# Two transformer blocks in one kernel: unscaled probabilities in the second attention, a new order in the delta rule, the conv products and the third pair's scores

## The reference

```python
# first block, delta rule, per head and chunk of 64 tokens
lower = bc[..., None] * jnp.einsum('nbhid,nbhjd->nbhij', kc, kc) * dec_strict
sol = lax.linalg.triangular_solve(lower + jnp.eye(C), rhs, left_side=True, lower=True, unit_diagonal=True)
...
o = rmsnorm(o, norm_w) * jax.nn.silu(z.reshape(B, S, H, dv))
# first block, sparse attention (8 heads, window, selected and compressed branches)
o = gates[..., 0:1] * o_cmp + gates[..., 1:2] * o_slc + gates[..., 2:3] * o_win
# second block
p = jax.nn.softmax(logits, axis=-1)              # 8 heads of 64, causal, with a bias by distance
attn_out = p @ v
u = a * jax.nn.sigmoid(g)                        # 512 channels
u = lax.conv_general_dilated(u, w_dw[:, None, :], ..., feature_group_count=C) + b_dw   # 31 taps, causal
mixed = jnp.concatenate([attn_out, layernorm_silu(u)], axis=-1)
h = h + mixed @ w_out[l]
```

## Time and profile before

| | us |
|---|---|
| median of three timed runs | 1605.27 (1605.24 to 1605.73) |
| profiled execution | 1607.56 |
| its span | 1605.8 |
| PE busy in the span | 1529.8 |
| DVE, ACT, POOL busy | 867.0, 641.9, 212.6 |

### The profile page before, as it was taken

The page is one execution under the profiler, slowest core; times in us unless marked ns, Lnnn a source line. Parts: engine busy times, 40 slices in busy tenths (PEclk is TensorE's granted clock), DMA queues, the critical chain, the costliest instruction groups (busy, mean ns, idle before and its releaser), DMA issues. The chain is left out here.

```text
span 1605.8 us, 21770 instructions
## 1 busy us (share of the span) xinstructions
PE 1529.8 (95%) x8438; PEld 1247.9 (78%) x8438; DVE 867.0 (54%) x1300; ACT 641.9 (40%) x936; POOL 212.6 (13%) x191
## 2 busy tenths in 40 slices
PE   6997999999999899999999998989799999999998
PEld 5777978667888777888888876767578888888886
DVE  5755446673444477766732266677626444444222
ACT  5354422463223244443422155454635444443221
POOL 0004000681000000000000001378610000000000
PEclk9999999999999999999999998999979999999999
DMA  5210032001223313233232233122103223222321
GB/s 211 79 53 16 2 142 101 21 1 40 98 93 110 105 53 103 81 104 104 69 115 90 91 123 105 53 79 79 30 24 105 91 92 104 99 83 73 104 94 71
DMA packets 22534, 132.17 MB, mean 82 GB/s; under 512 B 2480, under 2 KB 2864, under 8 KB 12224
## 3 DMA queue, kind: packets, MB, share of 16 engines
q1 hardware_dynamic: 20672, 123.48, 22.8%
q0 software_dynamic: 928, 6.36, 1.0%
q10 hardware_dynamic: 864, 1.36, 0.2%
HBM read 129.09 MB, written 2.10 MB: 82 GB/s over the span
## 5 line engine op out<-in xcount | busy, mean ns | idle before, releaser
L322 PE MATMUL ps<-AH,whi 128*128 128x512 f32 x1280 | 509.6, 398 | 39.1 <-DVE wlo L309 14.6
L323 PE MATMUL ps<-AL,whi 128*128 128x512 f32 x1280 | 504.8, 394 | 0.0
L324 PE MATMUL ps<-AH,wlo 128*128 128x512 f32 x1280 | 504.3, 394 | 0.0
L309 DVE TENSOR_TENSOR wlo<-raw,whi 128x2048 fp32r<-128x2048 f32 (+3 forms) x124 | 251.2, 2026 | 272.0 <-ACT whi L302 271.8
L322 PEld LDWEIGHTS ps<-AH,whi 128*128 128x128 f32 x1280 | 244.7, 191 | 95.9 <-issue 21.9
L324 PEld LDWEIGHTS ps<-AH,wlo 128*128 128x128 f32 x1280 | 244.3, 191 | 52.0
L323 PEld LDWEIGHTS ps<-AL,whi 128*128 128x128 f32 x1280 | 244.5, 191 | 50.4 <-issue 0.2
L302 ACT ACTIVATE whi<-raw 128x2048 fp32r<-128x2048 f32 (+3 forms) x124 | 210.3, 1696 | 169.9 <-PE ps L324 169.9
L322 PE MATMUL ps<-HH,whi 128*128 128x512 f32 x352 | 136.9, 389 | 0.0
L323 PE MATMUL ps<-HL,whi 128*128 128x512 f32 x352 | 136.9, 389 | 0.0
L324 PE MATMUL ps<-HH,wlo 128*128 128x512 f32 x352 | 136.9, 389 | 0.0
(11 more groups left out here) (384 smaller groups left out, 1928.9 us busy)
## 6 DMA issues: line engine op xcount, KB each, us to landing
raw<-wstream SPq DMA_DIRECT2D x78, 1024.0 KB, 4.8
raw<-wstream SPq DMA_DIRECT2D x32, 704.0 KB, 4.1
raw<-wstream SPq DMA_DIRECT2D x16, 768.0 KB, 4.3
hT<-xT SPq DMA_DIRECT2D x4, 512.0 KB, 7.9
raw<-wstream SPq DMA_DIRECT2D x4, 512.0 KB, 3.6
W1k<-w1k_d POOLq DMA_DIRECT2D x1, 2048.0 KB, 10.7
W1v<-w1v_d POOLq DMA_DIRECT2D x1, 2048.0 KB, 15.9
BT<-bias_d POOLq DMA_DIRECT2D x1, 1024.0 KB, 5.6
```

Of the source, the lines that this page charges most:

```text
L309: nc.vector.tensor_tensor(WL[b][:, 0:n], RAW[b][:, 0:n], WH[b][:, 0:n].bitcast(F32), ALU.subtract).then_inc(w_lo_done, 1)
L322: nc.tensor.matmul(out_, WH[b][:, w], xh[:, k, :], start=start and k == 0, stop=False)
L323: nc.tensor.matmul(out_, WH[b][:, w], xl[:, k, :], start=False, stop=False)
L324: last = nc.tensor.matmul(out_, WL[b][:, w], xh[:, k, :], start=False, stop=stop and k == n - 1)
```

## The change

1. Delta rule, start. POOL makes the masked copy of level 0 too (four more of L1077's kind, two to a tile and ahead of the query product), and DVE's two instructions become one subtraction, which stands one tile later.

```diff
+            def first_level(t):
+                dve.wait_ge(off_ready, 2 * t + 1)
+                vec.tensor_tensor(TTC[:, t, :, :], eye, OFFC[0][:, t, :, :], ALU.subtract).then_inc(tt_ready, 1)
+
...
-                dve.wait_ge(at_ready, t + 1)
-                own.link(vec.tensor_tensor(TTC[:, t, :, :], ATC[:, t, :, :], level, ALU.mult))
-                vec.scalar_tensor_tensor(TTC[:, t, :, :], TTC[:, t, :, :], -1.0, eye, ALU.mult, ALU.add).then_inc(tt_ready, 1)
+                if t:
+                    first_level(t - 1)
+            first_level(T - 1)
...
             for t in range(T):
+                pool.wait_ge(at_ready, t + 1)
+                offs(0, t)
+                offs(1, t)
                 qd = QKV[:, 0:GH, t * P:(t + 1) * P]
                 pool.wait_ge(row_exp, t + 1)
                 pool.wait_ge(qk_done, t + 1)
                 nc.gpsimd.tensor_tensor(qd, qd, Y1[:, t, :, :], ALU.mult).then_inc(qd_ready, 1)
-                pool.wait_ge(at_ready, t + 1)
-                offs(1, t)
```

```diff
-                if t >= 1:
+                if 0 < t < T - 1:
                     pe.wait_ge(yt_ready, t)
...
+            output(0)
             for t in range(T):
+                if t + 1 < T:
+                    if t:
+                        dve.wait_ge(yt_lo, t)
+                    output(t + 1)
+                dve.wait_ge(yt_hi, t + 1)
                 tok = slice(t * P, (t + 1) * P)
-                dve.wait_ge(ot_ps, t + 1)
-                tmp = TMP[:, t % 2, :].rearrange("p (h n) -> p h n", h=GH)
-                if t >= 2:
-                    dve.wait_ge(yt_lo, t - 1)
-                vec.scalar_tensor_tensor(tmp, ps[:, 4 + t % 2, :].rearrange("p (h n) -> p h n", h=GH), col("gdn"),
-                                         ZS[:, :, tok], ALU.mult, ALU.mult).then_inc(yt_ready, 1)
-                dve.wait_ge(yt_hi, t + 1)
-                vec.tensor_tensor(YAL[:, :, tok], tmp, YAH[:, :, tok].bitcast(F32), ALU.subtract).then_inc(yt_lo, 1)
+                vec.tensor_tensor(YAL[:, :, tok], TMP[:, t % 2, :].rearrange("p (h n) -> p h n", h=GH),
+                                  YAH[:, :, tok].bitcast(F32), ALU.subtract).then_inc(yt_lo, 1)
```

```diff
-            return ps[:, 7 if c == 3 else 3 + c, :]
+            return CU[:, 3, :] if c == 3 else ps[:, 3 + c, :]
...
-                        act.wait_ge(last_tap_done, k - 1)
-                        ins = nc.scalar.mul(PT2[:, 0, k % 2, :], src, w)
+                        if k >= 4:
+                            act.wait_ge(last_tap_done, k - 3)
+                        ins = nc.scalar.mul(PT2[:, k // 2 % 2, k % 2, :], src, w)
...
-                products(5)
+                products((3, 7, 6, 4)[c])
             for p in range(NPIECE["qk2"]):
+                stage_hi(act, "qk2", p // 2, p % 2, p >= 2)
                 products(6)
-                stage_hi(act, "qk2", p // 2, p % 2, p >= 2)
             products(len(LATE_TAPS))
```

```diff
-                    pe.wait_ge(p2_scaled, 2 * p + b + 1)
+                    pe.wait_ge(p2_ready, 2 * p + b + 1)
...
-                    pe.wait_ge(y2_lo, q) if q else bank_read(pe, "v2", 3)
+                    pe.wait_ge(y2_scaled, q) if q else bank_read(pe, "v2", 3)
...
+                pe.wait_ge(rl2_ready, q + 1)
+                if q:
+                    pe.wait_ge(rows2_sb, q)
+                for h in range(0, NH, 2):
+                    for b in range(2):
+                        last = nc.tensor.matmul(ps[side(b), 7, h // 2 * P:(h // 2 + 1) * P],
+                                                RL2[:, q % 2, h + b:h + b + 1].to_broadcast([P, DK]), ident[:, :],
+                                                start=True, stop=True)
+                last.then_inc(rows2_ps, 1)
...
+                if i % PER_QT2 == 1 and i > PER_QT2:
+                    sum_rows(i // PER_QT2 - 1)
...
+            pe.wait_ge(rows2_sb, T)
...
+            def save_rows(q):
+                act.wait_ge(rows2_ps, q + 1)
+                nc.scalar.activation(SQ[:, 0, :], ps[:, 7, :], ACT.Copy).then_inc(rows2_sb, 1)
...
+            def factors(q):
+                dve.wait_ge(p2_ready, NH * (q + 1))
+                vec.reciprocal(RL2[:, q % 2, :], LS2[:, q % 2, :]).then_inc(rl2_ready, 1)
+
+            def scale(q):
+                dve.wait_ge(rows2_sb, q + 1)
+                dve.wait_ge(o3_ps, PER_QT2 * (q + 1))
+                vec.tensor_tensor(TMP[:, 1, :], ps[:, 6, :], SQ[:, 0, :], ALU.mult).then_inc(y2_scaled, 1)
...
-            for p in range(len(PAIRS2)):
-                n = (PAIRS2[p][0] + 1) * P
-                pool.wait_ge(rl2_ready, p + 1)
-                for b in range(2):
-                    x = PR2[:, p % 3, b, 0:n]
-                    nc.gpsimd.tensor_scalar(x, x, RL2[:, p % 4, b:b + 1], None, ALU.mult).then_inc(p2_scaled, 1)
```

The rest of the order on DVE and ACT in that loop:

```diff
-                if i >= PER_QT2 + 3 and i % PER_QT2 == 3:
-                    save_hi(i // PER_QT2 - 1) if i < ITER2[-1] else None
                 if i < len(PAIRS2):
                     probabilities(i)
+                if i >= PER_QT2 + 3 and i % PER_QT2 == 3:
+                    save_hi(i // PER_QT2 - 1)
                 if i - 2 < len(PAIRS2):
                     for b in range(2):
                         save_pairs(act, nc.scalar.copy, i - 2, b)
+                if i % PER_QT2 == 1 and i > PER_QT2:
+                    save_rows(i // PER_QT2 - 1)
                 if i in (I_STAGE, I_STAGE + 2):
...
+                if i >= PER_QT2 + 3 and i % PER_QT2 == 3:
+                    scale(i // PER_QT2 - 1)
+                if i >= 2 * PER_QT2 and i % PER_QT2 == 0:
+                    save_lo(i // PER_QT2 - 2)
                 if i < len(PAIRS2):
...
-                if i - 1 < len(PAIRS2):
-                    factors(i - 1)
-                if i >= PER_QT2 + 3 and i % PER_QT2 == 3 and i < ITER2[-1]:
-                    save_lo(i // PER_QT2 - 1)
-                if i < len(PAIRS2):
                     top(i, 1)
+                if i >= PER_QT2 and i % PER_QT2 == 0:
+                    factors(i // PER_QT2 - 1)
...
+            scale(T - 1)
             save_lo(T - 1)
```

More of the change, by code:

```diff
@@ L970, in gdn_dve @@
             dve.wait_ge(gc_saved, 1)
-            level, eye = (CS[:, CON[x]:CON[x] + HB].unsqueeze(1).to_broadcast([P, GH, HB]) for x in ("level", "eye"))
+            eye = CS[:, CON["eye"]:CON["eye"] + HB].unsqueeze(1).to_broadcast([P, GH, HB])
+            def first_level(t):
+                dve.wait_ge(off_ready, 2 * t + 1)
+                vec.tensor_tensor(TTC[:, t, :, :], eye, OFFC[0][:, t, :, :], ALU.subtract).then_inc(tt_ready, 1)
             sums = lambda bank: ps[:, bank, :].rearrange("p (t h n) -> p t h n", t=T, h=GH)[:, :, :, 0]
@@ L1298, in nsa_pe @@
             nv_pe(pe, 1)
+            scores(2)
             pe.wait_ge(kv_c_sb, 1)
@@ L1414, in nsa_dve @@
             factors(0)
+            factors(1)
             dve.wait_ge(kv_c_ps, 1)
@@ L1819, in ple_dve @@
                     gather(dve, 4, m, b)
-        s2_ps, s2_max, p2_ready = (sem(n) for n in (
-            "s2_ps", "s2_max", "p2_ready"))
-        rl2_ready, p2_scaled, pt2_ps, o3_ps, y2_hi, y2_lo = (sem(n) for n in (
-            "rl2_ready", "p2_scaled", "pt2_ps", "o3_ps", "y2_hi", "y2_lo"))
+        p2_ready = sem("p2_ready")
+        rl2_ready, rows2_ps, rows2_sb, y2_scaled, pt2_ps, o3_ps, y2_hi, y2_lo = (sem(n) for n in (
+            "rl2_ready", "rows2_ps", "rows2_sb", "y2_scaled", "pt2_ps", "o3_ps", "y2_hi", "y2_lo"))
         pt2_sb = [sem(f"pt2_sb{b}") for b in range(2)]
@@ L1866, in scores @@
                     nc.tensor.matmul(ps[:, s2_bank(p, b), 0:n], QT2[side(b), h // 2, qt * P:n], KT2[side(b), h // 2, 0:n],
[L1867 removed]
+                                     start=True, stop=True).then_inc(s_ps, 1)
             def turn(p):
@@ L2142, in blk2_dve @@
             save_v(1)
-            factors(0)
             top(1, 0)
```

55 lines of the change are left out of this document (31 added, 24 removed).

## The result

The changed kernel takes 1583.74 us (median of 4 runs, 1581.50 to 1587.86), the kernel before 1605.5 beside it: a ratio of 0.9866, with a 95% interval of 0.9845 to 0.9887, which is 21.5 us less (18 to 25). The forecast was 1586.5, with 1582 to 1591 as its own range.

The account below looks back on a forecast made before the run. PE was taken as the bound, busy for 1529.8 of 1605.8 us. Terms -4.2 - 5.5 - 1.8 - 10.3 + 3.0 = -18.8 took 1607.56 to 1588.8; 2.3 lower for the median gave 1586.5 us, range 1582 to 1591.

Parts of the forecast that it names:

- The step: Delta rule's start: the last key product comes sooner, level 1 starts at 129.1 instead of 134.31; gain taken as 4.2 us.
- second rival: Delta rule's start: POOL holds all four subtractions, 1.38 us each; the gain shrinks to 1.2 us, time 1589.5; 12%.
- The circle: Delta rule's end: each turn waits 2.05 us over DVE, ACT and DVE; breaking it removes two PE idles of 1.39, 2.8 us.
- the clock term: Delta rule's end: PE's clock, 0.66 from 220 to 230, stays up if the gaps shrink, giving back 2.8 us.
- The 0.9 us of later waits: First attention: early pairs' row maxima, factors and POOL's scalings come earlier, so part of the later waits goes, 0.9 us.
- what is late next: Conv: DVE, 11.3 us from one `wlo` to the next against PE's 11.1; three pieces may wait 0.3 to 0.5 us each.
- third rival: Conv: DVE becomes the bound, seven pieces each wait 0.8 us for `wlo`; gain 5.5 to 6, time about 1591; 8%.
- the second is ACT's order: Conv: PE's 6.37 us wait for `wlo` at 1077.66 comes from staging behind eleven POOL-paced products; with four ahead it goes.
- The price of the rows: Second attention: four times 8 added PE matmuls, two groups at 1.03 and two at 2.06 us, 6.2 us in all.
- the gains of POOL and `y2_lo`: Second attention: PE's wait for the first scalings goes (1.0 us), and all but 0.5 of 2.8 us behind `y2_lo` (2.3).
- first rival: Second attention keeps the high clock since POOL's waits are gone: its term becomes -3 us, time 1580.5; 14%.
- the prediction's own mark: Channel sums behind the second attention expected at 1156.7; a start before 1151 or after 1161 would be wrong.

Follow-up runs that it names:

- `query_late`: Kernel before with POOL's four query products moved behind the loop over tiles; one execution, level 1 starts at 131.22 instead of 134.31, gain 2.3 us two steps on.
- `only_end`: Kernel before with the delta rule's end alone changed (next gate product ahead of the split, no wait behind the last turn): 0.9957, 6.9 us less.
- `stage_behind`: Changed kernel with each staging of qk2 again behind its six products; counts 3, 7, 6, 4 and four buffers stay: 0.9857 of before.
- `only_att2`: Kernel before with the second attention alone changed (probabilities unscaled, rows of reciprocals, sum of chunk 3 in SBUF): 0.9997 of before.
- `only_start`: Kernel before with the delta rule's start alone changed (POOL makes the level 0 mask, DVE subtracts): 0.9975, 4.0 us less.

## Why the prediction was right, part by part

The sum was right within 3 us. The sum of the five ratios alone is -4.0 - 6.9 - 2.6 - 9.8 - 0.5 = -23.8 us, and the whole -21.5 with an interval from -18 to -25: the parts add up.

**Delta rule, start: predicted 4.2, measured 4.0 (2.2 to 5.6).** The step was right, and the reason with it: POOL's query product holds up the DVE instruction, as `query_late` shows with 0.42 against 1.37. Of the second rival little came: the four subtractions took 0.41, 0.56, 0.56 and 0.94. Each of the three slower ones ends 0.28 us behind the POOL mask that was under way, so masks hold them just as the query product does, and they only meet less of it. Only the last one was held for long, and it stands behind the last key product. By the Trainium skill's rule ("GPSIMD Engine Reference", section 8) instructions with two SBUF inputs contend, and the trace agrees, with the numbers just given.

**Delta rule, end: predicted 5.5, measured 6.9 (4.7 to 9.0).** The circle broke as described. In the trace of `only_end` 5.3 us are won, 2.8 of them the two idles and 2.5 the clock; the 1.6 more in the ratio are within its interval, and no run shows a cause for them. The size of the clock term, 2.8, was read from one execution's window of 0.66. Of the six others with the same idles two come near it (0.66 and 0.70); in the other four half of the spell comes later.

**First attention: predicted 1.8, measured 2.6 (1.0 to 4.0), and 3.1 in the stretch.** This term was mis-sized in its kind. I priced one slow instruction, 2.06 against 1.13. The rows behind it were as slow, since the clock had fallen at the end of the narrow compressed scores (292.65) and stayed down until 299.5: five groups, 3.3 us of PE's time. In four of six executions the spell was half as long, and the five groups lost 1.7 us. The 0.9 us of later waits that I hoped for went the other way, 1.1 us more.

**Conv: predicted 10.3, measured 9.8 (7.1 to 12.5).** The sum held, and so did the guess on what is late next (1.0 us of waits for `wlo`; the third rival did not come). The step "the second is ACT's order" was wrong in its main part: four buffers instead of two, and one product fewer, brought the staging forward by 4.3 us and the wait down from 6.37 to 2.19, as `stage_behind` shows. That the sum came out near 10 all the same is luck in this part, since the edit held the order and the buffers together. I had named the pace of POOL, 1.43 us a product, but had not applied it to the number of buffers.

**Second attention: predicted +3.0, measured -0.5 (-3.2 to +2.4).** The price of the rows was nearly right (0.92 twice and 1.76 twice, 5.4 us; predicted 6.2), and the gains of POOL and `y2_lo` came (0.5 and 2.2). A new wait took their place: ACT's copies, 5.2 to 8.9. What failed is the clock in the sum: I priced two of the four groups at the low clock and took the rest of the stretch to keep the clock it had. It did not. With the old attention the clock over the stretch is 0.81 to 0.83 in all seven executions, with the changed one 0.84, 0.93 and 0.93. From the kernel before to `only_att2` PE's idle time in it grew from 8.9 to 10.3 us, and the stretch still became 2.5 us shorter, since PE was busy for 60.1 us instead of 63.9 with more matmuls. That it is the added rows which keep the clock up is argued and not shown: doubling them gave 0.91. The table shows two outcomes of the same attention, 70.3 and 74.75, on both sides of the old form's 71.6 to 73.5. So something near the first rival, 3 us less by the clock, happens in two of the three executions, and something near my forecast in the other.

**The profiled spans.** The channel sums stand at 1149.37, not at the predicted 1156.7; by the prediction's own mark (before 1151) that counts as wrong. Of these 7.3 us, 2.1 are that the profiled execution of before lay above its median (1607.56 against 1605.5), and 2.2 that the changed one lay below its own (1581.50 against 1583.74). The other 3.0 are the second attention and the delta rule's end. The two later sizes in the shifts, -6.6 for the start and 2.4 us behind the first attention, are of the same kind, differences between executions: from 360 and from 370 on, `only_start`, which leaves the first attention alone, shows a clock of 0.94 and 0.89 in windows of 10 us, the kernel before 1.00 and 0.66.

## What to carry to other kernels

Where PE is the bound, price a gap as its length plus the low clock behind it, and follow the slow rows until they end rather than pricing the first one. Work that is added to PE among waits can come with a higher clock, so the sum of its single rows need not be its price, and here the runs could not tell a price for 5.4 us of it. Two profiled executions do not give the sizes of small parts, even if every landmark is matched: put each part alone into the kernel before, and look at the same stretch in all executions. A paced producer in front of a needed instruction is worth asking how many buffers it has before its place in the list is blamed.
